# Three accumulator banks in turn for the samples' mLSTM state updates

## The chip, the cores and the metric

The kernel runs on one core of one Trainium2 chip. The metric is the device time of the kernel in microseconds, from the start of the launch to its end. The kernel before took 808.34 us, the median of three runs (807.4, 808.34 and 808.98).

## What is computed

One layer of a hybrid decoder, for a prompt of 256 tokens and for 8 samples of 8 new tokens each, in 32-bit floats. Each token goes through an mLSTM branch with 4 heads of 256 features and a forgetting-attention branch with 8 heads of 128. The branches are merged, and a mixture of 32 gated experts follows. The part that matters here is the mLSTM of the samples. Each of the 8 samples has, for each of the 4 heads, a state matrix C of 256 x 256 with a normaliser vector n beside it; the kernel holds the two as one 256 x 257 matrix, in two halves of 128 rows. The reference computes for it

```
num = w_inter[..., None] * jnp.einsum('bhtd,bhde->bhte', q, C) + jnp.einsum('bhts,bhse->bhte', s, v)
...
C_new = decay_state[..., None, None] * C + jnp.einsum('bhs,bhsd,bhse->bhde', w_rows, k, v)
```

That is, each of the 32 pairs of sample and head needs a query times state product, a key times value product (the update) and a read and a write of its state in memory.

## The kernel before, in words

Projections, attention and mLSTM pieces are interleaved by hand. The projections with `w_in` and the branch matrices are cut into 48 chunks of 256 columns and each chunk into 2 or 3 units; `dense` (lines 1808 to 1851) issues the matmuls of a unit. `stages()` (lines 74 to 137) attaches small pieces, called stages here, to units: after unit `(c, u)` each engine runs the stages in `AT[c, u]`, in the order of that list. PE, ACT and DVE each walk the same list in program order.

The samples' mLSTM consists of these stages, for head h and sample b:
- `SA(h)`: PE computes the scores of head h into bank 3 (`scores`, line 1934), DVE multiplies them by the decay weights (L1399), and ACT scales the keys (L989, L991) and masks them for the first sample (L998).
- `SB(h, b)`, called a step below, is numbered n = 8h + b. PE multiplies the masked queries by the sample's state and adds into bank 5 (L1995, two products). Then it computes the two halves of the update, into one bank each (L2006). DVE takes each half with one instruction, new state = decay x old state + bank (L1420), 128 x 257 elements each, and a tiny memset (L1422) signals that both are done. ACT masks the keys for the next step (L998), as soon as PE is through the step before.
- At the head's last sample, b = 7, PE also computes the scores times values product (L2001) between the two. ACT takes the upper half of bank 5 (L1008). DVE lays out the next head's queries (L1406), does its two L1420, adds the halves of bank 5 (L1425) and adds the product of L2001 (L1428).

The steps do not all come in a row: the 32 of them are spread over nine lines of the list, each behind one dense unit of the section `ga` (or the first unit of `gb`), with 4, 4, 3, 4, 3, 4, 3, 4 and 3 steps. `SA(h + 1)` follows `SB(h, 7)` directly, on every engine. The group of steps between two dense units is called a burst here. The first burst holds steps 0 to 3, the second 4 to 7, then 8 to 10, 11 to 14, 15 to 17, 18 to 21, 22 to 24, 25 to 28 and 29 to 31. Head ends (steps 7, 15 and 23, each followed by an `SA`) fall in bursts 2, 5 and 7; in bursts 5 and 7 the next head's first step follows in the same burst, in burst 2 a dense unit does. Burst 2 also holds the stages F2H and F2L of the prompt, which use bank 3 too.

PSUM has 8 banks. Dense units take banks 0 to 2 in turn, bank 3 holds scores, bank 5 query times state. PE claims a bank by waiting until its reader has let it go:

```
def claim(st, b):

    if fill[st, b]:
        pe.wait_ge(sem(f"bank_free{b}"), fill[st, b])
```

`fill[st, b]` is the number of earlier stages in the whole list that use bank b, counted from `banks_of(st)` (line 140). In `SB` the update banks are 6 and 7 for every step, and L2001 writes bank 4. `pe_past(st)` waits for the last bank in `banks_of(st)`.

The states move through rings in SBUF: four buffers `Cin` for the old states and four `Cout` for the new ones. All these transfers are issued on the POOL queue, 257 KB each: after step n (`cout_full`), first the load of the state for step n + 4 (L702) and then the store of the state of step n (L714). PE waits for the load at the head of a step (line 1993), DVE waits before step n + 4 until the store of n has landed (line 1414). The dense weights come on the SP queue, 1 MB a chunk.

Of the kernel before, what the change touches and what calls it, by code (L numbers as in the profile page):

```python
# [18 lines left out]
ALU = mybir.AluOpType  # L19
# [11 lines left out]
TP, BS, TS = 256, 8, 8  # L31
NS = BS * TS
# [3 lines left out]
HM, DM = 4, 256  # L36
DE = DM + 1
# [99 lines left out]
    return at  # L137


def banks_of(st):  # L140

    kind, x, y = st
    if kind == "G":
        return {1: (3,), 2: (4, 5, 6), 3: (3, 7), 4: (3, 7, 4, 5, 6), 5: (3,)}[x]
    if kind == "P2":
        return (4, 6, 7) if x == 0 else (5, 4, 6, 7)
    if kind == "SB":
        return ((5, 4) if y == BS - 1 else ()) + (6, 7)
    return {"KT": (6, 7), "P1": (3,), "F1": (), "F3": (), "F2": (6, 7), "F2H": (3,), "F2L": (), "SA": (3,), "N1": (), "N2": (6, 7),
            "FP1": (7, 4), "FP2": (5,), "FP3": (6,), "FS1": (3,), "FS2": (5,), "FS3": (3,), "FS4": (3,), "FS0": (),  # L150
            "FPN": (), "FSN": ()}[kind]
# [19 lines left out]
def hybrid_step(nc, A, O):  # L171
# [3 lines left out]
    for c in range(NCH):  # L175
        for u in range(units_of(c)):
            for st in AT[c, u]:
                for b in banks_of(st):
                    fill[st, b] = count[b]
                    count[b] += 1  # L180
    ctx = ExitStack()
    with ctx:
        handles = {}

        def sem(name):
            if name not in handles:
                
                handles[name] = ctx.enter_context(nc.semaphore(name))
            return handles[name]
# [15 lines left out]
        bank = [ctx.enter_context(nc.psum_tensor(f"bank{b}", [P, 512], F32)) for b in range(8)]  # L205
# [6 lines left out]
        def take(n):  # L212
            top[0] += n
            assert top[0] <= FW, top[0]
            return fm[:, top[0] - n:top[0]]

        def cube(ap, a):
            return ap.rearrange("p (a b) -> p a b", a=a)
# [18 lines left out]
        ew = cube(take(48), 3)  # L237
# [31 lines left out]
        num = cube(take(HM * DE), HM)  # L269
        qm = take(2 * BS * DIAG)  # L270
        SW = [take(128) for _ in range(2)]
        kw = [take(DM) for _ in range(2)]
        kwm = [take(DM) for _ in range(2)]
        inter = take(DE)
# [122 lines left out]
        def vx(t, h, w=DE):  # L397
            return vx01[:, t, h, 0:w] if t < 2 else vx2[0:NS, h, 0:w]
# [196 lines left out]
        def _(pool):  # L595
# [57 lines left out]
            def pe_past(st):  # L653

                b = banks_of(st)[-1]
                pool.wait_ge(sem(f"bank_full{b}"), fill[st, b] + 1)
# [168 lines left out]
        def _(act):  # L825
# [7 lines left out]
            def pe_past(st):  # L833

                b = banks_of(st)[-1]
                act.wait_ge(sem(f"bank_full{b}"), fill[st, b] + 1)
# [330 lines left out]
        def _(dve):  # L1167
            s = Steps(dve, sem("dve_step"))
            v = nc.vector
            TT, TSC, STT, CP = v.tensor_tensor, v.tensor_scalar, v.scalar_tensor_tensor, v.tensor_copy  # L1170

            def got(st, b):

                dve.wait_ge(sem(f"bank_full{b}"), fill[st, b] + 1)
# [6 lines left out]
            def done(ins, b):  # L1181
                s(ins, sem(f"bank_free{b}"))
# [221 lines left out]
            def lay_queries(h):  # L1404
                for k in range(2):
                    s(CP(diag(qm[:, 576 * k:576 * (k + 1)]), qT[:, 2 * h + k, TP:NT].rearrange("p (b t) -> p b t", t=TS)),  # L1406
                      sem("qm_full"))

            def SB(st):
                _, h, b = st  # L1410
                n = h * BS + b
                if n >= NCOUT:

                    dve.wait_ge(sem(f"cout_out{n % NCOUT}"), 16 * (n // NCOUT))
                if b == BS - 1 and h < HM - 1:
                    got(st, 5)
                    lay_queries(h + 1)
                for k, bk in enumerate((6, 7)):
                    got(st, bk)
                    done(STT(Cout[n % NCOUT][:, k, :], Cin[n % NCIN][:, k, :], dec8[:, HM * b + h:HM * b + h + 1],  # L1420
                             bank[bk][:, 0:DE], ALU.mult, ALU.add), bk)
                s(v.memset(small[0:1, 94:95], 0.0), sem("cout_full"))  # L1422
                if b == BS - 1:
                    dve.wait_ge(sem("inter_upper"), h + 1)
                    TT(inter[0:NS, :], bank[5][0:NS, 0:DE], inter[0:NS, :], ALU.add).then_inc(sem("bank_free5"), 1)  # L1425
                    dve.wait_ge(sem("bank_free5"), fill[st, 5] + 1)
                    got(st, 4)
                    done(STT(num[0:NS, h, :], inter[0:NS, :], ew[0:NS, 2, h:h + 1], bank[4][0:NS, 0:DE],  # L1428
                             ALU.mult, ALU.add), 4)
                    s(v.memset(small[0:1, 94:95], 0.0), sem("num_full"))  # L1430
                    s(v.memset(small[0:1, 94:95], 0.0), sem("inter_used"))

# [99 lines left out]
            def FS4(st):  # L1532
# [4 lines left out]
                s(v.memset(small[0:1, 94:95], 0.0), sem("o_full"))  # L1537

            run = dict(G=G, P1=P1, P2=P2, F1=F1, F2=F2, F2H=F2H, F2L=F2L, F3=F3, SA=SA, SB=SB, N1=N1, FP1=FP1,
                       FPN=FPN, FP3=FP3, FS0=FS0, FS1=FS1, FSN=FSN, FS2=FS2, FS3=FS3, FS4=FS4)  # L1540

# [254 lines left out]
        def _(pe):  # L1796
            mm = nc.tensor.matmul
            n_act = units(SECTIONS.index("bm") * CPS)[0]
# [6 lines that stand above are left out]
            def full(ins, b):  # L1805
                ins.then_inc(sem(f"bank_full{b}"), 1)
# [48 lines left out]
            for n in range(6):  # L1855
# [5 lines left out]
                for i in range(4):  # L1861
                    k = 4 * half + i
# [6 lines left out]
            for k in range(KC):  # L1869
                for i, (w, a) in enumerate(((0, 0), (0, 1), (1, 0))):  # L1870
                    ins = mm(bank[7][0:16, 0:NT], wgs[w][:, k, :], r1[a][:, k, :], start=(k == 0 and i == 0),
                             stop=(k == KC - 1 and i == 2))
# [114 lines left out]
            def SB(st):  # L1987
                _, h, b = st
                n = h * BS + b
                if b == 0:  # L1990
                    claim(("SB", h, BS - 1), 5)
                    pe.wait_ge(sem("qm_full"), 2 * (h + 1))
                pe.wait_ge(sem(f"cin_in{n % NCIN}"), 16 * (n // NCIN + 1))
                for k in range(2):
                    ins = mm(bank[5][NS * k:NS * (k + 1), 0:DE], qm[:, 576 * k + 64 * b:576 * k + 64 * (b + 1)],  # L1995
                             Cin[n % NCIN][:, k, :], start=(b == 0), stop=(b == BS - 1), skip_group_check=True)
                if b == BS - 1:
                    full(ins, 5)
                    pe.wait_ge(sem("bank_free3"), fill[("SA", h, 0), 3] + 1)
                    claim(st, 4)  # L2000
                    full(mm(bank[4][0:NS, 0:DE], SW[(2 * HM + h) % 2][0:NS, 0:64], vx(2, h), start=True, stop=True), 4)  # L2001
                pe.wait_ge(sem("kwm_ready"), n + 1)
                for k, bk in enumerate((6, 7)):
                    claim(st, bk)
                    rows = slice(NS * k, NS * (k + 1))
                    full(mm(bank[bk][:, 0:DE], kwm[n % 2][rows, 0:P], vx2[rows, h, :], start=True, stop=True), bk)  # L2006
# [91 lines left out]
            def FS4(st):  # L2098
# [3 lines left out]
                full(nc.tensor.transpose(bank[3][:, 0:P], Ob, ident), 3)  # L2102

            run = dict(G=G, KT=KT, P1=P1, P2=P2, F2=F2, F2H=F2H, SA=SA, SB=SB, N2=N2, FP1=FP1, FP2=FP2, FP3=FP3,
                       FS1=FS1, FS2=FS2, FS3=FS3, FS4=FS4)
            def turn(cc):
# [49 lines left out]
            for t in range(3):  # L2156
# [12 lines left out]
               start=False, stop=True, skip_group_check=True).then_inc(sem("router_full"), 1)  # L2169
# [192 lines left out]
```

## Time and profile before

| | us |
|---|---|
| median of 3 runs | 808.34 |
| the profiled execution, whole | 806.17 |
| its span in the trace | 804.6 |
| PE matmuls busy in the span | 712.9 (89%) |
| DVE busy | 392.5 (49%) |
| ACT busy | 294.7 (37%) |

The table reads as one kernel with several stretches: the dense sections in front keep PE busy, the experts at the end stream 96 MB of weights. The samples' steps lie between 204.9 and 287.8 us of the span. In the rows further below, a row of a timeline has the start in us, the duration in us, engine, line, operation, what is written and read, and how often; in brackets stands how long the engine had been idle before and what ended that. Two or more instructions of one line are merged into one row. One matmul of 32-bit floats makes two records, so "x4" is two products.

### The profile page before, as it was taken

How to read it: one execution, taken by the hardware profiler on the slowest of the kernel's cores; microseconds unless marked ns; L12 is line 12 of the kernel's file. 1: busy time of each engine (PE TensorE's matmuls, PEld its weight loads, DVE VectorE, ACT ScalarE, POOL GpSimd, SP SyncE). 2: the span in 40 equal slices, each digit the busy share in tenths (PEclk: the TensorE clock that was granted, in tenths of full speed). 3: DMA queues.
4: the chain of work that ended last, by engine and by line, in shares of the span. 5: the costliest groups of instructions: out<-in, count | busy, mean ns of one | idle time of the engine just before them, and what ended most of it. 6: DMA issues, size and time to landing. Idle time of an engine off the chain costs nothing.

```text
span 804.6 us, 14412 instructions
## 1 busy us (share of the span) xinstructions
PE 712.9 (89%) x5462; PEld 570.0 (71%) x5462; DVE 392.5 (49%) x865; ACT 294.7 (37%) x530; POOL 141.1 (18%) x247
## 2 busy tenths in 40 slices
PE   2999899999999999898899999895999999887880
PEld 1799899999666689898788899784565555443430
DVE  3475423456755453848477768648632222111123
ACT  5433544365533354546433354435221111111110
POOL 6000100000343300042243110000113223121210
PEclk9999999999999999999999999996999999999996
DMA  5342443332899944372798748926999999999975
GB/s 200 105 156 107 143 158 105 115 109 93 264 253 263 249 140 164 106 237 95 261 320 280 253 152 362 380 99 237 358 419 419 419 419 418 421 418 420 419 324 207
DMA packets 38186, 202.57 MB, mean 252 GB/s; under 512 B 7443, under 2 KB 7971, under 8 KB 18915
## 3 DMA queue, kind: packets, MB, share of 16 engines
q1 hardware_dynamic: 23938, 158.98, 51.2%
q0 software_dynamic: 13744, 41.32, 16.5%
q10 hardware_dynamic: 432, 1.31, 0.4%
q8 instruction: 46, 0.75, 0.4%
q14 instruction: 26, 0.21, 0.1%
HBM read 184.24 MB, written 23.12 MB: 258 GB/s over the span
## 4 chain that ended last, share of the span: by engine, by line
PE 65%; DMA 14%; DVE 12%; ACT 5%; issue 3%; SPq 1%; DVEq 0%; ACTq 0%; POOL 0%; POOLq 0%
PE bank L1844 22%; PE bank L1848 10%; PE bank L2208 9%; DMA fm<-in_w_moe 7%; PE bank L2228 4%; PE bank L1834 4%; DMA em<-in_w_moe 4%; DVE rm L1187 3%; PE bank L2006 2%; ACT rm L846 2%; PE bank L2092 1%; PE bank L1995 1%; PE bank L2180 1%; DMA fm<-y_rows 1%; DMA out_C_sample<-fm 1%
## 5 line engine op out<-in xcount | busy, mean ns | idle before, releaser
L1844 PE MATMUL bank<-rm 128*128 128x320 f32 x1344 | 206.0, 311 | 2.6 <-ACT fm L874 1.6
L1844 PEld LDWEIGHTS bank<-rm 128*128 128x128 f32 x1344 | 197.4, 188 | 7.3 <-issue 3.9
L1187 DVE TENSOR_TENSOR rm<-fm,rm 128x2048 fp32r<-128x2048 f32 x48 | 110.1, 2293 | 70.4 <-ACT rm L846 69.8
L1848 PE MATMUL bank<-rm 128*128 128x256 f32 x960 | 120.8, 284 | 2.4 <-DVE fm L1586 2.4
L1848 PEld LDWEIGHTS bank<-rm 128*128 128x128 f32 x960 | 116.9, 191 | 3.3 <-issue 2.9
L2208 PE MATMUL bank<-fm,em 128*64 128x256 f32 x368 | 93.7, 401 | 17.5 <-DMA fm<-in_w_moe 15.3
L846 ACT ACTIVATE rm<-fm 128x2048 fp32r<-128x2048 f32 x48 | 92.1, 1919 | 16.8 <-PE bank L1844 10.6
L2208 PEld LDWEIGHTS bank<-fm,em 128*64 128x64 f32 x368 | 49.5, 142 | 53.7 <-issue 31.5
L2210 PE MATMUL bank<-fm,em 128*64 128x256 f32 x320 | 82.6, 405 | 0.0
L1145 ACT ACTIVATE fm<-bank 64x256 f32<-64x256 f32 x32 | 12.0, 376 | 137.1 <-PE bank L2210 137.1
L778 POOL DMA_INDIRECT y_rows<-fm,im x32 | 28.9, 903 | 166.1 <-DVE fm L1741 166.1
L702 POOL DMA_DIRECT2D fm<-in_state_C x32 | 17.6, 551 | 164.4 <-DVE fm L1341 119.2
L2210 PE MATMUL bank<-em 128*64 128x256 f32 x192 | 46.3, 384 | 0.0
L2210 PEld LDWEIGHTS bank<-fm,em 128*64 128x64 f32 x320 | 43.3, 143 | 0.0
L1746 DVE TENSOR_TENSOR fm<-bank,fm 64x256 f32<-64x256 f32 x32 | 13.6, 426 | 60.7 <-ACT fm L1145 60.7
L1834 PE MATMUL bank<-rm 128*128 128x256 f32 x320 | 42.9, 286 | 0.0
L1420 DVE SCALAR_TENSOR_TENSOR fm<-fm,bank 128x257 f32<-128x257 f32 x64 | 28.0, 480 | 30.1 <-PE bank L2006 28.8
L1762 DVE COPY fm<-bank 128x128 f32<-128x128 f32 x32 | 9.3, 292 | 65.2 <-PE bank L2219 65.2
L1834 PEld LDWEIGHTS bank<-rm 128*128 128x128 f32 x320 | 40.0, 191 | 1.7 <-DVE fm L1586 1.0
L2208 PE MATMUL bank<-em 128*64 128x256 f32 x144 | 34.6, 383 | 2.8 <-DMA em<-in_w_moe 2.8
L2228 PE MATMUL bank<-em,fm 128*64 128x512 f32 x144 | 34.0, 593 | 1.5 <-issue 0.9
L1741 DVE COPY fm<-bank 64x512 f32<-64x512 f32 x32 | 22.2, 694 | 26.9 <-PE bank L2228 26.9
(400 smaller groups left out, 942.2 us busy)
## 6 DMA issues: line engine op xcount, KB each, us to landing
fm<-in_w_moe SPq DMA_DIRECT2D x57, 1024.0 KB, 22.1
fm<-in_w_dense SPq DMA_DIRECT2D x48, 1024.0 KB, 4.9
em<-in_w_moe SPq DMA_DIRECT2D x39, 1024.0 KB, 27.3
fm<-in_state_C POOLq DMA_DIRECT2D x32, 257.0 KB, 5.6
out_C_sample<-fm POOLq DMA_DIRECT2D x32, 257.0 KB, 6.7
fm<-in_cache_kT POOLq DMA_DIRECT2D x16, 512.0 KB, 6.8
fm<-in_cache_v POOLq DMA_DIRECT2D x8, 512.0 KB, 5.7
em<-in_cache_v POOLq DMA_DIRECT2D x8, 512.0 KB, 7.8
```

What stands on the lines that cost most here:

```text
L702: pool.dma_start(Cin[n % NCIN], A["state_C"][n % BS, n // BS]).then_inc(sem(f"cin_in{n % NCIN}"), 16)
L778: pool.indirect_dma_start(y_rows, bass.IndirectOffsetOnAxis(ap=row_i[:, v:v + 1].bitcast(U32), axis=0), yrow[v % NY], None, bounds_check=6 ...
L846: s(A_(pair[c % 2][0], cube(raw[c % RAW1], KC), ACT.Copy), sem("hi_done"))
L1187: s(TT(pair[c % 2][1], cube(raw[c % RAW1], KC), pair[c % 2][0], ALU.subtract), sem("split_done"))
L1420: done(STT(Cout[n % NCOUT][:, k, :], Cin[n % NCIN][:, k, :], dec8[:, HM * b + h:HM * b + h + 1], bank[bk][:, 0:DE], ALU.mult, ALU.add), bk)
L1741: CP(yrow[v % NY][:, D // 2:D], bank[4 + v % 2][CAP:2 * CAP, :]).then_inc(sem("e_y_right"), 1)
L1834: ins = mm(bank[b][:, 0:CW], samp[:, k, :], w[:, k, :], start=(k == 0 and i == 0), stop=(k == KC - 1 and i == 1))
L1844: ins = mm(bank[b][:, 0:NT], w[:, k, P * u:P * (u + 1)], a[:, k, :], start=first, stop=final)
L1848: ins = mm(bank[b][0:r, 0:CW], a[:, k, TILE0[u]:TILE0[u] + r], w[:, k, :], start=first, stop=final)
L2208: last_g = mm(bank[b][0:CAP, 0:FE], x[:, k, :], g[:, k, :], start=(k == 0), stop=(k == KC - 1), skip_group_check=True)
L2210: last_u = mm(bank[b][CAP:2 * CAP, 0:FE], x[:, k, :], u[:, k, :], start=(k == 0), stop=(k == KC - 1), skip_group_check=True)
L2228: ins = mm(bank[b][CAP * j:CAP * (j + 1), :], hT[:, k, :], w[:, k, 512 * j:512 * (j + 1)], start=(k == 0), stop=(k == 1), skip_group_check ...
```

## The change

In `banks_of` and in the `SB` of PE and DVE, the update of step n takes banks (6, 7), (4, 6) or (7, 4), by n modulo 3. The score times value product of a head's last step goes to bank 3 in place of bank 4. Nothing else is changed: the same instructions, sizes, transfers and order.

```diff
@@ -137,6 +137,11 @@
+def update_banks(h, b):
+
+    return ((6, 7), (4, 6), (7, 4))[(h * BS + b) % 3]
...
@@ -145,7 +150,7 @@
     if kind == "SB":
-        return ((5, 4) if y == BS - 1 else ()) + (6, 7)
+        return ((5, 3) if y == BS - 1 else ()) + update_banks(x, y)
...
@@ -1415,7 +1420,7 @@
-                for k, bk in enumerate((6, 7)):
+                for k, bk in enumerate(update_banks(h, b)):
                     got(st, bk)
...
@@ -1424,9 +1429,9 @@
-                    got(st, 4)
-                    done(STT(num[0:NS, h, :], inter[0:NS, :], ew[0:NS, 2, h:h + 1], bank[4][0:NS, 0:DE],
-                             ALU.mult, ALU.add), 4)
+                    got(st, 3)
+                    done(STT(num[0:NS, h, :], inter[0:NS, :], ew[0:NS, 2, h:h + 1], bank[3][0:NS, 0:DE],
+                             ALU.mult, ALU.add), 3)
...
@@ -1997,10 +2002,10 @@
                 if b == BS - 1:
                     full(ins, 5)
                     pe.wait_ge(sem("bank_free3"), fill[("SA", h, 0), 3] + 1)
-                    claim(st, 4)
-                    full(mm(bank[4][0:NS, 0:DE], SW[(2 * HM + h) % 2][0:NS, 0:64], vx(2, h), start=True, stop=True), 4)
+                    claim(st, 3)
+                    full(mm(bank[3][0:NS, 0:DE], SW[(2 * HM + h) % 2][0:NS, 0:64], vx(2, h), start=True, stop=True), 3)
                 pe.wait_ge(sem("kwm_ready"), n + 1)
-                for k, bk in enumerate((6, 7)):
+                for k, bk in enumerate(update_banks(h, b)):
                     claim(st, bk)
```

## Rows read from the trace of the kernel before

**Rows 1.** Window of all steps: length, PE, PEld, DVE, ACT, POOL busy, clock, DMA share, GB/s.
```profile
204.90:287.80 82.90, 78.53 (x478) 50.82 (x477) 46.66 (x135) 34.00 (x63) 32.02 (x59) 1.00 0.90 255
```

**Rows 2.** Waits of PE in that stretch: us in total, times, longest.
```profile
PE bank L1995 <- DVE fm L1425: 2.4, 2, 1.3
PE bank L2006 <- DVE fm L1420: 1.0, 6, 0.2
```

**Rows 3.** Timeline of PE, the third burst (steps 8 to 10).
```profile
226.12 0.65 PE L1995 MATMUL bank<-fm 128*64 128x257 f32 x4
226.70 0.70 PE L2006 MATMUL bank<-fm 64*128 64x257 f32 x4
227.34 0.65 PE L1995 MATMUL bank<-fm 128*64 128x257 f32 x4
228.16 1.00 PE L2006 MATMUL bank<-fm 64*128 64x257 f32 x4 [0.17 <-DVE fm L1420]
229.09 0.65 PE L1995 MATMUL bank<-fm 128*64 128x257 f32 x4
```

**Rows 4.** Timeline of DVE, the first of these steps.
```profile
227.53 0.88 DVE L1420 SCALAR_TENSOR_TENSOR fm<-fm,bank 128x257 f32<-128x257 f32 x2 [2.86 <-PE bank L2006]
```

**Rows 5.** Timeline of PE: the first step, and the dense unit behind each burst.
```profile
204.88 0.66 PE L1995 MATMUL bank<-fm 128*64 128x257 f32 x4
...
210.77 3.79 PE L1844 MATMUL bank<-rm 128*128 128x320 f32 x24
...
222.40 3.79 PE L1844 MATMUL bank<-rm 128*128 128x320 f32 x24
...
230.52 3.79 PE L1844 MATMUL bank<-rm 128*128 128x320 f32 x24
...
240.19 3.79 PE L1844 MATMUL bank<-rm 128*128 128x320 f32 x24
...
250.40 3.79 PE L1844 MATMUL bank<-rm 128*128 128x320 f32 x24
...
260.06 3.79 PE L1844 MATMUL bank<-rm 128*128 128x320 f32 x24
...
279.25 3.78 PE L1844 MATMUL bank<-rm 128*128 128x320 f32 x24
...
287.73 4.46 PE L1848 MATMUL bank<-rm 128*128 128x256 f32 x35
```

**Rows 6.** Timeline of DVE at the first head's end, and of PE there.
```profile
223.72 0.47 DVE L1428 SCALAR_TENSOR_TENSOR fm<-fm,bank 64x257 f32<-64x257 f32 x1
...
222.02 0.45 PE L1934 MATMUL bank<-fm 128*64 128x64 f32 x4
```

**Rows 7.** Busy time by window: before that head end.
```profile
211.50:224.40 12.90, 12.20 (x80) 8.13 (x80) 11.82 (x31) 7.98 (x13) 5.27 (x10) 1.00 0.96 280
```

**Rows 8.** Timeline at the second and third head's end: DVE and PE.
```profile
245.56 0.43 DVE L1406 COPY fm<-fm 128x64 f32<-128x64 f32 x2 [4.09 <-DMA out_C_sample<-fm]
...
247.41 0.47 DVE L1428 SCALAR_TENSOR_TENSOR fm<-fm,bank 64x257 f32<-64x257 f32 x1
...
247.43 0.65 PE L1995 MATMUL bank<-fm 128*64 128x257 f32 x4 [1.28 <-DVE fm L1425]
...
268.37 0.65 PE L1995 MATMUL bank<-fm 128*64 128x257 f32 x4 [1.13 <-DVE fm L1425]
```

**Rows 9.** Issue to landing: all stores (L714), then the load of step 14 (L702).
```profile
DMA to landing us min/median/max: 3.3/6.7/9.2
...
L702 POOL DMA_DIRECT2D fm<-in_state_C x1: 546/546/546, 231.7 to 231.7; - x1
DMA to landing us min/median/max: 7.0/7.0/7.0
```

**Rows 10.** Busy time, granted clock and DMA share by window: two quarters of the stretch.
```profile
226.00:247.00 21.00, 19.74 (x120) 12.72 (x118) 9.74 (x28) 8.23 (x17) 7.58 (x14) 1.00 0.91 247
268.00:288.00 20.00, 19.28 (x116) 12.57 (x117) 9.62 (x28) 6.80 (x12) 7.03 (x13) 1.00 0.79 234
```

## The prediction, made before the changed kernel was run

> **What bounds the kernel now.** I read the window of the steps first [rows 1]: of 82.9 us PE is busy in 78.5, at full clock, while DVE has 46.7 and ACT 34.0. So this stretch goes by PE, and what follows it is dense work on PE, so a microsecond won at its end should move all that comes later. But the same row has the 16 DMA engines busy for a share of 0.90. The second thing to see is that there are two suspects, PE's waits and the state transfers.
>
> The waits of PE [rows 2] name DVE's L1420, the reader of banks 6 and 7, with only 1.0 us in 6 waits. That is too small: a wait between the two products of a step hides in a longer "busy" row. The timeline shows it [rows 3]. Step 8 finds both banks free: 0.58 us from its start to its L2006 (226.12 to 226.70), 0.64 more to the next step, so a plain step is 1.22 us. Step 9 takes 1.75 us (227.34 to 229.09): its L2006 starts 0.24 us later than plain and is 1.00 us long in place of 0.70. DVE starts on the first bank 0.83 us after that L2006 started (226.70 to 227.53), is through both at 228.41, and PE goes on 0.63 us after DVE's start, at 228.16 [rows 3, 4].
>
> How much is that over all bursts? A dense unit holds PE for 3.72 us (230.52 to 234.24, where burst 4 starts), so a burst's length is the difference of two dense rows less 3.72 [rows 5]. Burst 1: 210.77 - 204.88 = 5.89 for 4 steps, against 4.88 plain: 1.01 held. Burst 3: 230.52 - 222.40 - 3.72 = 4.40 against 3.66: 0.74. Burst 4: 9.67 - 3.72 = 5.95 against 4.88: 1.07. Burst 5, behind the head's end at 247.43 [rows 8], 2.97 against 2.44 for 2 steps: 0.53. Burst 6: 9.66 - 3.72 = 5.94: 1.06. Burst 8 starts one plain step and one dense unit behind 268.37 [rows 8], at 273.31, and ends at 279.25: 1.06. Burst 9: 287.73 - 282.97 = 4.76 against 4.23 (a head's last step is 0.57 longer, for L2001): 0.53. Bursts 2 and 7 have no hold by these banks. Sum: **6.0 us**, all on PE's path.
>
> **Part 1, three banks.** Step n + 1 takes first a bank that step n doesn't use, then the first bank of step n. PE has that one back 0.83 + 0.63 = 1.46 us after step n's L2006 started [rows 3, 4], and wants it at 1.22 + 0.32 (half of the 0.64) = 1.54. It fits, by 0.1 us. Step n + 2 wants step n's second bank at 2.44; it is free at 0.83 + 0.88 + about 0.15 = 1.86. DVE has 0.88 us of work per step of 1.22. ACT's mask for step n + 2 starts when step n is through. So I take all 6.0 us of holds as removed, with 0 to 6.0 as ends. No instruction is added.
>
> **Part 2, bank 3, is a new wait.** Before, L2001's product lay in bank 4, and SA of the next head, right behind on PE, wrote its scores to bank 3, long free. Now SA's `claim` counts this use of bank 3 too: PE can't issue L1934 until DVE has read the product in L1428, the last of DVE's reading work for the head, behind L1406, both L1420 and L1425. Queued behind on PE are a dense unit (head 0) or the next head's first step (heads 1 and 2). Head 3 has no SA behind it.
> - Head 0: PE's L1934 started at 222.02, L1428 ended at 223.72 + 0.47 = 224.19 [rows 6]. DVE was busy 11.8 of the 12.9 us before [rows 7], so its end can't be drawn forward by PE; it starts this run of work 0.7 us earlier, though, since burst 1 is 1.0 us shorter (the square root on ACT in between keeps the rest). L1428 ends at 223.5, L1934 starts at 223.6: PE is **1.6 us later** than before. The hold of burst 1 is swallowed by this too: PE's earlier arrival only waits longer.
> - Heads 1 and 2: PE already waited there for bank 5, let go by L1425, until 247.43 and 268.37 (1.28 and 1.13 us idle, [rows 8]). L1428 ends at 247.41 + 0.47 = 247.88; then L1934 still has to run, 0.38 us (222.02 to 222.40, [rows 5, 6]), and only then the next step: 248.36 in place of 247.43, **0.93 us later**, twice. Between nothing (if the old wait covered it) and 1.3 us (all DVE's tail), I take 0.93, since the order on both queues is fixed.
>
> **Part 3, the transfers answer.** A load for step n + 4 is issued when step n is done, and lands 7.0 us later for step 14 (issued at 231.7, so at 238.7 [rows 9]; it is the last step of burst 4, which ends at 240.19 [rows 5], so it could hardly begin before). Bursts shorter by 1.0 us eat that slack. In burst 3 PE starts 1.6 later and ends 1.6 - 0.74 = 0.84 later; the load for step 14 goes out about 1.0 later and lands at 239.7, where a plain burst 4 wants it at 230.52 + 0.84 + 3.72 + 3 x 1.22 = 238.74. So burst 4 gives its gain back: it ends at 239.7 + 1.22 = 240.94, 0.75 later than before in place of 0.2 earlier. Next, DVE's L1406 at head 1's end waited for the store of step 11 (4.09 us, [rows 8]), which now goes out 0.84 later: DVE is 0.84 late there, and the step behind it 0.84 + 0.93 = 1.8 late, 0.1 more than PE's own sum.
>
> The sum, as PE's lateness against before: +1.6 after head 0, +0.84 after burst 3, +0.75 after burst 4, +1.75 behind head 1's end, +1.2 after the rest of burst 5 (-0.53), +0.15 after burst 6 (-1.06), +1.1 behind head 2's end, 0.0 after burst 8 (-1.06), **-0.5** at 287.7 (-0.53). Behind it nothing is changed. The profiled execution was 806.17 us; this makes 805.7, and against the median, 808.34, 2.2 us above it, **807.9 us**.
>
> **A rule weighed.** The trace has the same hold in 7 of 9 bursts on the engine that should be saturated [rows 3, 5]. The Trainium skill (Perfetto Trace Analysis, Optimization Strategy) says that a gap which repeats so can mean too little PSUM for the next tile. By it the change would be worth the whole 6.0 us; the trace agrees on the cause, and the new wait on bank 3 is what the rule doesn't see. On the transfers, the row has 3.3 to 9.2 us from issue to landing for 257 KB [rows 9]. The Trainium skill (DMA: Bandwidth & Descriptors, Anatomy of one DMA) gives 2.0 us and the size over 436 GB/s, an estimate of 2.6 us alone. The trace doesn't agree, since the queue is full here; by that figure part 3 would be nothing and the forecast 1.0 us lower.
>
> **The rivals.** 0.2% of this time, 1.6 us, is about what a measurement of this kernel can tell from no change.
> - *The transfers keep up*, because the share of 0.91 to 0.79 [rows 10] leaves room: only parts 1 and 2. From the +1.6 after head 0: -0.74 - 1.07 + 0.93 - 0.53 - 1.06 + 0.93 - 1.06 - 0.53 = -1.5, so 806.8 us. Add that DVE's tail at the head ends comes earlier than I think, by 0.3 each, and it is 2.4 us faster, 805.9. For it: the share falls to 0.79 at the end. Chance 0.2.
> - *All 6.0 us of holds come through*, 802.3 us: this needs DVE to have done L1428 before PE reaches the SA, and [rows 6, 8] show it 2.2 us (224.19 against 222.02) behind. The rule on repeating gaps above would have it so. Chance 0.02.
> - *The state queue sets the pace*, slower than before: 514 KB a step, with the share at 0.91 [rows 10] and landings up to 9.2 us [rows 9] against four buffers. Then bursts 4 to 6 gain nothing, since each step waits for the load issued four steps earlier, and the three head ends stand: 1.6 + 0.93 + 0.93 - 0.74 - 1.06 - 0.53 = +1.1 with bursts 3, 8 and 9 still gaining, +1.9 without burst 3, so 809.4 to 810.2 us. It decides from landings that are 0.5 us later, after their issue, than before. Chance 0.18.
> - *The change doesn't do what it says*: the fit of 0.1 us fails, a step is still held by DVE. Then L1428 ends at 224.19 as before, and PE is 2.2 late at head 0: 2.2 + 0.93 + 0.93 = +4.1, 812.4 us. Chance 0.03.
>
> **How the numbers follow.** The forecast's own case has 0.57, with 807.0 to 808.9. Beyond the 1.6 us on the fast side lies about half and a little more of the first rival, the second, and a few hundredths of the forecast: faster 0.2. On the slow side the last rival, half of the one on the state queue and a few hundredths: slower 0.17. Same 0.63. The range for 8 in 10 takes in most of the first rival and most of the state queue's: 806.2 to 809.9.
>
> **What would show it.** In the changed profile L2006 of every step should be 0.70 us and the steps of bursts 1, 3 and 6 1.22 us apart. PE should be idle 1.5 to 2.2 us before L1934 at head 0's end and 1.8 at the other two, released by L1428. Burst 4 should have a wait of about 1 us for a state load, and DVE's wait for a store at head 1's end should stay near 4 us. Rows of L2006 of 1.00 us would refute part 1; an L1934 that doesn't wait for L1428, part 2; a burst 4 of 4.9 us, part 3. A stretch that ends before 286 would make the number wrong.

## The result, and the profile of the changed kernel

The changed kernel takes **819.43 us** (median of 4 runs, 817.78 to 821.72), against 807.87 for the kernel before in the same session. The ratio is 1.014, with an interval of 1.0115 to 1.0165: 11.6 us slower, where no measurable change was forecast. The profiled execution took 819.31 us, its span 817.8; in the text below every difference between traces is between single executions.

The stretch of the steps grew from 82.85 us (204.88 to 287.73, [rows 5]) to 94.64 (204.26 to 298.90), by 11.8. So the loss lies there. Behind it the changed trace is 2.0 us longer as well (518.9 against 516.9 us to the end of the span): it has one more stretch of low clock, 42 us behind the steps, that the other trace lacks. In front it is 0.6 us shorter. The two profiled executions are 13.1 us apart, the medians 11.6. First the timeline of PE in the changed kernel (start, duration, engine, line, operation, count, idle time and its end in brackets). Its lines are 5 higher than before: L2000 is the query times state product, L2011 the update, L1939 the next head's scores, L1849 and L1853 dense units.

```profile
204.26 0.65 PE L2000 MATMUL bank<-fm 128*64 128x257 f32 x4
204.85 0.70 PE L2011 MATMUL bank<-fm 64*128 64x257 f32 x4
205.48 0.66 PE L2000 MATMUL bank<-fm 128*64 128x257 f32 x4
206.07 0.82 PE L2011 MATMUL bank<-fm 64*128 64x257 f32 x4
...
209.37 3.79 PE L1849 MATMUL bank<-rm 128*128 128x320 f32 x24
...
220.33 0.70 PE L2011 MATMUL bank<-fm 64*128 64x257 f32 x4 [0.56 <-ACT fm L1003]
223.31 0.69 PE L1939 MATMUL bank<-fm 128*64 128x64 f32 x4 [2.28 <-DVE fm L1433]
223.93 6.03 PE L1849 MATMUL bank<-rm 128*128 128x320 f32 x24
229.89 0.66 PE L2000 MATMUL bank<-fm 128*64 128x257 f32 x4
...
233.69 3.78 PE L1849 MATMUL bank<-rm 128*128 128x320 f32 x24
...
241.84 0.65 PE L2000 MATMUL bank<-fm 128*64 128x257 f32 x4 [0.57 <-DMA fm<-in_state_C]
...
251.68 0.39 PE L1939 MATMUL bank<-fm 128*64 128x64 f32 x3 [3.04 <-DVE fm L1433]
...
255.58 4.07 PE L1849 MATMUL bank<-rm 128*128 128x320 f32 x24
259.58 0.65 PE L2000 MATMUL bank<-fm 128*64 128x257 f32 x4
...
264.74 3.79 PE L1849 MATMUL bank<-rm 128*128 128x320 f32 x24
...
270.69 0.65 PE L2000 MATMUL bank<-fm 128*64 128x257 f32 x4 [0.94 <-DMA fm<-in_state_C]
...
276.88 0.58 PE L1939 MATMUL bank<-fm 128*64 128x64 f32 x3 [4.33 <-DVE fm L1433]
...
279.51 5.59 PE L1849 MATMUL bank<-rm 128*128 128x320 f32 x24
285.04 0.65 PE L2000 MATMUL bank<-fm 128*64 128x257 f32 x4
...
290.20 3.78 PE L1849 MATMUL bank<-rm 128*128 128x320 f32 x24
...
298.90 1.33 PE L1853 MATMUL bank<-rm 128*128 128x256 f32 x9
```

Three things are to be seen. The bursts are shorter: the first takes 209.37 - 204.26 = 5.11 us, where it took 5.89 [rows 5], and the third 233.69 - 229.89 = 3.80 in place of 4.40. Then L1939 stands behind DVE's L1433 for 2.28, 3.04 and 4.33 us, where PE was idle for 0, 1.28 and 1.13 [rows 8]. And the next dense unit takes 6.03, 4.07 and 5.59 us in place of 3.79, for the same 24 records; at the second and third head end a step or two stand between the wait and the unit.

The windows of the changed kernel behind the three waits say why (length, busy time of PE, PEld, DVE, ACT and POOL, then granted clock, DMA share, GB/s):

```profile
223.30:230.00 6.70, 6.69 (x30) 6.38 (x32) 0.34 (x3) 0.00 (x0) 0.37 (x1) 0.58 0.72 155
251.60:256.40 4.80, 4.72 (x23) 2.34 (x24) 1.94 (x9) 2.31 (x2) 1.52 (x3) 0.64 0.60 143
276.80:285.00 8.20, 8.12 (x36) 6.55 (x36) 3.52 (x8) 0.00 (x0) 1.52 (x3) 0.59 0.56 141
```

The granted clock is 0.58, 0.64 and 0.59 of full speed: PE ran for most of each at 1.2 GHz in place of 2.4, where the kernel before had 1.00 over the whole stretch [rows 1]. What happened before each fall was an idle PE.

DVE's side at the third head end of the changed kernel:

```profile
270.56 1.00 DVE L1425 SCALAR_TENSOR_TENSOR fm<-fm,bank 128x257 f32<-128x257 f32 x2 [4.89 <-DMA out_C_sample<-fm]
271.50 0.06 DVE L1427 MEMSET fm<- 1x1 f32 x1
274.41 0.43 DVE L1411 COPY fm<-fm 128x64 f32<-128x64 f32 x2 [2.85 <-issue]
274.87 0.88 DVE L1425 SCALAR_TENSOR_TENSOR fm<-fm,bank 128x257 f32<-128x257 f32 x2
275.80 0.06 DVE L1427 MEMSET fm<- 1x1 f32 x1
275.89 0.42 DVE L1430 TENSOR_TENSOR fm<-bank,fm 64x257 f32<-64x257 f32 x1
276.35 0.47 DVE L1433 SCALAR_TENSOR_TENSOR fm<-fm,bank 64x257 f32<-64x257 f32 x1
```

DVE waits for the store of step 18 to land, then idles 2.85 us more, put down to "issue". The kernel makes DVE wait there for the store of step 19. It was issued at 264.07 and landed 10.3 us later, at 274.4, which is when DVE goes on. All of DVE's tail (2.4 us) is behind that, and PE's scores behind the tail.

**Where the 11.8 us came from.** From the last L2011 of a head to the step behind the next dense unit: 9.56 in place of 4.73 us at head 1's end (220.33 to 229.89 against 221.39 to 226.12), 11.65 against 9.06 at the second, 13.19 against 7.14 at the third: 13.5 in all. Of that, idle time before L1939 or the next step is 9.65 - 2.41 = 7.2, and the rest, 6.2, together with 0.5 of bank holds that went, is the low clock: 6.58 for L1939 and a dense unit in place of 4.10, 7.90 in place of 6.54 for the second, 8.16 in place of 5.32 for the third, 6.7 in all. Waits of PE for state loads cost 0.6, 1.0 and 0.75 us in bursts 4, 7 and 9, against 0.1. The other bursts gave back 4.4 us. 13.5 + 2.4 - 0.1 - 4.4 leaves 0.4 of the 11.8 for small moves in burst 2.

### The profile page after: what moved, and what is told of

It reads as the page before. It is cut to its first block, busy times and chain, and to the rows that moved or that the text cites. A ratio compares the mean times of both kernels' runs of the same rounds, so it can differ in the third digit from the quotient of the medians.

```text
span 817.8 us, 14412 instructions
## 1 busy us (share of the span) xinstructions
PE 717.2 (88%) x5462; PEld 573.3 (70%) x5462; DVE 393.2 (48%) x865; ACT 294.5 (36%) x530; POOL 140.9 (17%) x247
## 4 chain that ended last, share of the span: by engine, by line
PE 64%; DMA 15%; DVE 11%; ACT 4%; issue 3%; SPq 1%; POOL 1%; DVEq 0%; ACTq 0%; POOLq 0%
PE bank L1849 21%; PE bank L1853 11%; PE bank L2213 9%; DMA fm<-in_w_moe 7%; PE bank L2233 4%; PE bank L1839 4%; DMA em<-in_w_moe 3%; DVE rm L1192 2%; DMA out_C_sample<-fm 2%; ACT rm L851 2%; PE bank L2097 1%; PE bank L2011 1%; PE bank L2185 1%; PE bank L2000 1%; DMA fm<-y_rows 1%
## 5 line engine op out<-in xcount | busy, mean ns | idle before, releaser
L1849 PE MATMUL bank<-rm 128*128 128x320 f32 x1344 | 210.3, 316 | 2.6 <-ACT fm L879 1.6
L1849 PEld LDWEIGHTS bank<-rm 128*128 128x128 f32 x1344 | 201.7, 192 | 8.0 <-issue 4.5
L1853 PE MATMUL bank<-rm 128*128 128x256 f32 x960 | 122.4, 287 | 2.4 <-DVE fm L1591 2.4
L1853 PEld LDWEIGHTS bank<-rm 128*128 128x128 f32 x960 | 118.4, 194 | 3.3 <-issue 2.9
L2213 PE MATMUL bank<-fm,em 128*64 128x256 f32 x368 | 92.4, 397 | 17.4 <-DMA fm<-in_w_moe 15.3
L851 ACT ACTIVATE rm<-fm 128x2048 fp32r<-128x2048 f32 x48 | 92.1, 1919 | 17.3 <-PE bank L1849 10.5
L2215 PE MATMUL bank<-fm,em 128*64 128x256 f32 x320 | 81.2, 400 | 0.0
L1839 PEld LDWEIGHTS bank<-rm 128*128 128x128 f32 x320 | 40.0, 191 | 1.7 <-DVE fm L1591 1.0
```

Of the source, the lines that this page charges most:

```text
L851: s(A_(pair[c % 2][0], cube(raw[c % RAW1], KC), ACT.Copy), sem("hi_done"))
L1839: ins = mm(bank[b][:, 0:CW], samp[:, k, :], w[:, k, :], start=(k == 0 and i == 0), stop=(k == KC - 1 and i == 1))
L1849: ins = mm(bank[b][:, 0:NT], w[:, k, P * u:P * (u + 1)], a[:, k, :], start=first, stop=final)
L1853: ins = mm(bank[b][0:r, 0:CW], a[:, k, TILE0[u]:TILE0[u] + r], w[:, k, :], start=first, stop=final)
L2213: last_g = mm(bank[b][0:CAP, 0:FE], x[:, k, :], g[:, k, :], start=(k == 0), stop=(k == KC - 1), skip_group_check=True)
L2215: last_u = mm(bank[b][CAP:2 * CAP, 0:FE], x[:, k, :], u[:, k, :], start=(k == 0), stop=(k == KC - 1), skip_group_check=True)
```

## The experiments

They ran in three sessions; each ratio is to the kernel before in the same one, so differences between runs of different sessions are best taken from the ratios. The last two columns are of the one profiled execution: its time, and the length of its stretch from the first step to the dense unit behind the last. Where that execution lies far from the median (it was the slowest of its kernel in e2, e5 and e11), the length says less about the median.

| run | us | ratio (interval) | profiled, us | stretch, us |
|---|---|---|---|---|
| the change | 819.43 | 1.014 (1.0115 to 1.0165) | 819.31 | 94.6 |
| e1 product in bank 3, two update banks | 814.46 | 1.0075 (1.0058 to 1.0092) | 813.70 | 90.0 |
| e2 three update banks, product apart | 807.40 | 0.9988 (0.9972 to 1.0003) | 810.24 | 83.6 |
| e3 change, scores a step earlier | 809.43 | 1.0029 (1.0002 to 1.0057) | 807.31 | 83.2 |
| e4 change, PE kept busy in the waits | 809.60 | 1.0026 (1.0004 to 1.0048) | 809.64 | 85.4 |
| e5 change, half stores | 810.12 | 1.0036 (1.0016 to 1.0055) | 814.50 | 89.2 |
| e6 before, half stores | 806.76 | 0.9981 (0.9965 to 0.9997) | 808.23 | 82.7 |
| e7 three banks, product apart, half stores | 803.96 | 0.9952 (0.9932 to 0.9972) | 804.45 | 80.2 |
| e8 as e2, PE kept busy at head ends | 806.89 | 0.9986 (0.9965 to 1.0006) | 807.22 | 83.0 |
| e9 as e4, first head end only | 811.18 | 1.0052 (1.003 to 1.0074) | 809.99 | 86.2 |
| e10 change, stores on SP | 815.39 | 1.011 (1.0073 to 1.0146) | 814.50 | 90.3 |
| e11 before, stores on SP | 806.57 | 1.000 (0.9983 to 1.0017) | 812.26 | 87.4 |
| e12 as e2, stores on SP | 806.95 | 1.0004 (0.9983 to 1.0024) | 806.99 | 82.7 |

### Each part alone: e1 and e2

e1 undoes the first part of the change:

```diff
 def update_banks(h, b):
-    return ((6, 7), (4, 6), (7, 4))[(h * BS + b) % 3]
+    return (6, 7)
```

> Only the second part of the change: the updates stay in banks 6 and 7 in turn, the score times value product goes to bank 3. Theory A (the slowdown is PE's wait at the three head ends for the product's reader, DVE's last instruction, plus the half granted clock that follows a wait of over 2 us): the loss stays, without the gain of three banks, so 816 to 825 us, with waits of L1939 on L1433 of 2 to 4 us at the head ends and a granted clock near 0.5 behind at least two of them. Rival B (three update banks, or bank 4 itself, disturb the bursts): as before the change, 807 to 810 us.

Measured: ratio 1.0075, so the loss is there with the second part alone, though smaller than expected (814.46 us, under the 816 that was the lower end). Its waits of L1939 and the windows behind them:

```profile
224.16 0.69 PE L1939 MATMUL bank<-fm 128*64 128x64 f32 x4 [2.15 <-DVE fm L1433]
224.78 6.13 PE L1849 MATMUL bank<-rm 128*128 128x320 f32 x24
...
252.50 0.39 PE L1939 MATMUL bank<-fm 128*64 128x64 f32 x3 [2.01 <-DVE fm L1433]
...
256.22 4.27 PE L1849 MATMUL bank<-rm 128*128 128x320 f32 x24
...
275.17 0.39 PE L1939 MATMUL bank<-fm 128*64 128x64 f32 x3 [2.02 <-DVE fm L1433]
...
276.62 3.79 PE L1849 MATMUL bank<-rm 128*128 128x320 f32 x24
```
```profile
224.00:231.00 7.00, 6.84 (x30) 6.54 (x32) 0.44 (x4) 0.00 (x0) 0.52 (x1) 0.57 0.60 169
252.50:256.50 4.00, 4.00 (x21) 1.87 (x22) 1.35 (x7) 2.31 (x2) 1.45 (x3) 0.68 0.52 139
275.00:280.40 5.40, 5.23 (x38) 4.32 (x40) 3.62 (x8) 1.55 (x1) 1.61 (x3) 1.00 0.82 200
```

The waits are 2.0 to 2.15 us at all three head ends, and the clock falls behind two of them. The third is as long as the second, and there the clock stays at 1.00. The stretch is 7.1 us longer than before.

e2 is the first part alone. The product needs a place where nothing waits for it: the upper 64 partitions of bank 3, since the scores use the lower 64. The Trainium skill (PSUM — Partial Sum Buffer, PSUM bank collisions raise a hardware error) says that two engines may use one bank at a time if they are in different groups of 32 partitions; no run here tests where that ends, but this one relies on it.

```diff
-                    claim(st, 3)
-                    full(mm(bank[3][0:NS, 0:DE], SW[(2 * HM + h) % 2][0:NS, 0:64], vx(2, h), start=True, stop=True), 3)
+                    if h == 0:
+                        pe.wait_ge(sem("bank_free3"), fill[("F2H", 1, 1), 3] + 1)
+                    else:
+                        pe.wait_ge(sem("num_full"), 2 * HM + h)
+                    mm(bank[3][NS:2 * NS, 0:DE], SW[(2 * HM + h) % 2][0:NS, 0:64], vx(2, h), start=True, stop=True)
...
-        return ((5, 3) if y == BS - 1 else ()) + update_banks(x, y)
+        return ((5,) if y == BS - 1 else ()) + update_banks(x, y)
```

DVE reads `bank[3][NS:2 * NS, 0:DE]`.

> Only the first part: three update banks in turn, and the product in the upper 64 partitions of bank 3, where the next head's scores don't have to wait for it. Theory A: no wait of L1939 on L1433, no half clock, and most of the 6.0 us of holds gone: 802 to 806 us. Rival B (bank rotation disturbs): 815 to 820 us. Rival C (the state transfers set the pace in any case): 806.5 to 809 us, with waits of PE for state loads and of DVE for stores that grow by what the holds lose.

Measured: 0.9988. The loss is gone, so three banks and bank 4 do no harm by themselves. But the 6 us aren't there either; that is rival C. PE in e2, where L1999 is the query times state product:

```profile
242.14 0.65 PE L1999 MATMUL bank<-fm 128*64 128x257 f32 x4 [0.26 <-DMA fm<-in_state_C]
...
246.44 1.12 PE L1999 MATMUL bank<-fm 128*64 128x257 f32 x4 [2.07 <-DVE fm L1430]
...
264.96 0.65 PE L1999 MATMUL bank<-fm 128*64 128x257 f32 x4 [0.74 <-DMA fm<-in_state_C]
...
286.02 0.65 PE L1999 MATMUL bank<-fm 128*64 128x257 f32 x4 [1.13 <-DMA fm<-in_state_C]
```

PE waits 2.4 us in all for state loads, and the old wait for bank 5 at the second head end is 2.07 us in place of 1.28 (DVE waits for a store ahead of it, as before the change), with a granted clock of 0.58 over the 4 us behind it. The clock fell once more at 287.3, 1.3 us behind the start of the row at 286.02, ahead of which PE had waited 1.13 us for a load. This trace is of the slowest of ten executions; the median is 2.8 us lower.

The two parts don't add: the second alone costs 0.75%, the first alone nothing, both 1.4%.

### The order alone: e3

```diff
+            if b == BS - 1 and h < HM - 1:
+                line.append(("SA", h + 1, 0))
             line.append(("SB", h, b))
...
-        if h < HM - 1:
-            line.append(("SA", h + 1, 0))
```

> The whole change, but the next head's scores (SA) are put ahead of the head's last step in the hand-written order, so that they no longer stand behind the product in bank 3. Theory A: as the run with the product apart, 802 to 806 us; a short wait of PE for bank 3 ahead of the product (up to 0.5 us, three times) is possible. Rival B: 815 to 820 us. Rival C: 806.5 to 809 us.

Measured: 1.0029. All of the change is kept but the scores' place, and 9 of the 11.6 us come back. It isn't the 802 to 806 of theory A: PE now waits for bank 3 ahead of the product, 2.0 us in 2 waits (behind DVE's L1404), more than the 0.5 each that I had allowed, and twice for bank 5, 1.50 and 1.60 us. Behind the second of these the granted clock was 0.61 for 4.1 us. The ten executions spread more than those of other runs, from 805.63 to 815.38 us; the profiled one, at 807.31, is among the fast.

### The clock: e4, e9 and e8

In e4 PE computes something that nobody reads while it would wait, into the bank that the next dense unit overwrites:

```diff
             def SA(st):
                 _, h, _ = st
+                if h:
+                    c, u = at_unit
+                    n = units(c)[0] + u + 1
+                    m = n - NRING
+                    pe.wait_ge(sem("unit_free_a"), m + 1 - thirds(m))
+                    for _ in range((3, 4, 4)[h - 1]):
+                        mm(bank[n % NRING][:, 0:NT], ident, fm[:, 0:NT], start=True, stop=True)
                 claim(st, 3)
```

> The whole change, with 3, 4 and 4 matmuls that nobody reads (128x320, about 0.6 us each) on PE ahead of the wait at the three head ends, so that PE is busy while it would be idle. They compute nothing of the output. Theory A (both wait and clock count): the wait itself stays, the granted clock stays at full level, and the 6.7 us that the trace shows lost at the lower level come back: 811 to 814 us. Theory A' (only the wait counts, the clock fell for another reason): 818 to 821 us, with the clock still at half behind the head ends. If the wait for the product were not the cause, more work on PE would only add: 820 us or more.

Measured: 1.0026. With eleven added matmuls the kernel is 9.2 us faster by the ratios (809.60 against 819.43 us). Their record (L1995), the scores and the dense unit behind them at the first head end, and the windows at all three:

```profile
221.49 1.88 PE L1995 MATMUL bank<-fm 128*128 128x320 f32 x6
223.84 0.45 PE L1939 MATMUL bank<-fm 128*64 128x64 f32 x4 [0.47 <-DVE fm L1433]
224.21 3.79 PE L1849 MATMUL bank<-rm 128*128 128x320 f32 x24
```
```profile
221.50:228.00 6.50, 6.03 (x38) 4.95 (x38) 2.42 (x10) 1.37 (x4) 1.53 (x3) 1.00 0.94 306
247.00:256.00 9.00, 9.00 (x56) 6.42 (x56) 6.29 (x15) 3.79 (x6) 3.25 (x6) 1.00 0.61 161
267.80:275.60 7.80, 7.62 (x48) 5.73 (x46) 5.73 (x14) 3.33 (x5) 2.96 (x6) 1.00 0.70 171
```

PE still can't issue L1939 before L1433: it starts 19.05 us behind the first step in both traces. So the order costs what it did, but the clock is 1.00 and the dense unit 3.79 us. The gain is larger than the 6.7 us of low clock: at the other two head ends L1939 came within 0.2 us behind 2.42 us of such matmuls, where it had waited 3.04 and 4.33. So there is a follow-on.

e9 is e4 with `if h == 1` in place of `if h`, that is, at the first head end only.

> The whole change with the matmuls that nobody reads (3) only in the wait at the first head end; at the other two PE idles as in the changed kernel. If the late landings of the stores (waits of 3.0 and 4.3 us at heads 2 and 3 in place of about 2) come from what the low clock behind the first head end did to the bunching of the bursts: 811 to 813.5 us, waits of L1939 near 2.0 us at both. If they come from shorter bursts alone: waits of 3 us and more stay, 814 to 817 us.

Measured: 1.0052, by the ratios 7 us better than the change, by keeping one wait busy whose own low clock had cost 2.5. L1939 waits 3.04 us at the second head end, as in the change, and 2.10 at the third in place of 4.33; the clock is 0.61 behind the second and 1.00 behind the third. Neither expectation held whole: the time fits the first, the second wait the other. The late stores at the third head end went with the first fall of the clock, those at the second didn't. The fall alone doesn't make them late either: e1, with two update banks, has it too (0.57), and its third wait is 2.02 us.

e8 puts two such matmuls behind the scores at head ends 2 and 3 of e2.

> Three update banks with the product apart, whole stores, and at head ends 2 and 3 two matmuls that nobody reads (1.3 us) behind the next head's scores, where PE otherwise idled 2.1 and 1.2 us for bank 5 and the clock fell behind the first of these. The theory: no low clock in the stretch of the steps, about 1.5 us less than the run with the product apart: 805 to 807 us. If that fall of the clock cost nothing or has another cause: 807 to 809 us.

Measured: 0.9986, against 0.9988 for e2. The clock was full at both head ends, but fell once elsewhere, behind a wait of 1.55 us for a state load in burst 4. So 806.89 us lies in the expected range, but no gain over e2 is shown.

### The transfers: e5, e6 and e7

The three store only the first half of each new state:

```diff
-                pool.dma_start(O["C_sample"][n % BS, n // BS], Cout[n % NCOUT]).then_inc(sem(f"cout_out{n % NCOUT}"), 16)
+                pool.dma_start(O["C_sample"][n % BS, n // BS][:, 0, :], Cout[n % NCOUT][:, 0, :]).then_inc(sem(f"cout_out{n % NCOUT}"), 16)
```

> The changed kernel, with the store of each new state cut to its first half (128 rows x 257, 128.5 KB in place of 257); the second half is not written to memory. The theory (late landings of the stores make DVE late at head ends 2 and 3, so they lengthen PE's new wait from the 1.8 us that order alone gives to 3.0 and 4.3, and set off the low clock): waits of L1939 at heads 2 and 3 of 1.5 to 2.1 us, no wait of DVE for a store, 811 to 815 us; the first head's wait (2.3 us) and its low clock stay. If landings don't matter: waits as in the changed kernel, 817 to 820 us.

> The control: the kernel before, with the same halved stores. In its profile the stores' landing holds DVE 4.1 and 1.1 us and through it PE at two head ends by up to 1.3 us each. The theory: 805 to 807.5 us. If transfers were what sets the whole stretch: 803 us or less.

> Three update banks with the product apart (upper 64 partitions of bank 3), and halved stores. The theory (three banks do remove 6 us of holds on PE, but the transfers, near their limit, give them back as waits for loads and stores): now the gain shows, 800.5 to 804 us, 2.5 us or more under the kernel before with halved stores, with the waits of PE for state loads (2.4 us in 4 with whole stores) under 0.5 us. If the holds are given back elsewhere (DVE or ACT): 804.5 to 807 us.

Measured: e5 1.0036, e6 0.9981, e7 0.9952. In e5 no wait of DVE for a store is left, and L1939 waits 2.28, 2.02 and 2.11 us: order alone. The median, 810.12 us, is a little under the range. The profiled execution is the slowest of the ten, with the clock low behind all three waits (0.56, 0.66 and 0.75), so its stretch of 89.2 us is longer than most would be. The kernel before gains 0.2% by the same cut (e6), within what was expected if transfers don't set its stretch. And now three banks are worth something: e7 is 2.8 us under e6, with every run of it (802.79 to 804.56) under every run of e6 (804.58 to 808.28), no wait of PE for a load, and this burst 4 (start at 232.41, next dense unit at 237.57), 5.16 us for four steps:

```profile
232.41 0.66 PE L1999 MATMUL bank<-fm 128*64 128x257 f32 x4
...
237.57 3.79 PE L1848 MATMUL bank<-rm 128*128 128x320 f32 x24
...
264.62 0.93 PE L1999 MATMUL bank<-fm 128*64 128x257 f32 x4 [1.33 <-DVE fm L1430]
265.47 1.23 PE L2013 MATMUL bank<-fm 64*128 64x257 f32 x4
266.63 4.52 PE L1848 MATMUL bank<-rm 128*128 128x320 f32 x24
```

It lost some 1.5 us again to the clock, which fell behind a wait of 1.33 us for bank 5: from 264.62 the step and the dense unit take 6.46 us, where 1.22 + 3.72 is plain.

### Another queue: e10, e11 and e12

The stores are issued from SP, ahead of the load of the dense chunk that its program comes to after the same bursts:

```diff
+            def states_out(c):
+                for u in range(units_of(c)):
+                    for st in AT[c, u]:
+                        if st[0] == "SB":
+                            n = stored[0]
+                            sp.wait_ge(sem("cout_full"), n + 1)
+                            sp.dma_start(O["C_sample"][n % BS, n // BS], Cout[n % NCOUT])\
+                                .then_inc(sem(f"cout_out{n % NCOUT}"), 16)
+                            stored[0] += 1
...
             for c in range(RAW1, NCH):
+                if c - RAW1 >= 2:
+                    states_out(c - RAW1 - 2)
```

> The changed kernel with the stores of the new states issued from the SP queue, among the dense weights' loads, in place of the POOL queue, whose order held each load and store one behind the other. Same bytes. If the single POOL queue is what makes landings late: waits of DVE for stores under 2 us in all, L1939 waits near 2.0, 811 to 814 us. If the DMA engines themselves are full: 815 to 820 us.

> The kernel before with its stores on the SP queue: the control. Its head ends wait for a store once (4.1 us of DVE): 806 to 808 us if the queue is the cause of that, 807.5 to 810 us if the engines are full.

> Three update banks, the product apart in the upper 64 partitions of bank 3, and the stores on the SP queue: the candidate for a version faster than both. If the POOL queue's order is the limit: 803 to 806 us, as with halved stores. If the DMA engines are: 806.5 to 809 us, as with the stores on POOL.

Measured: 1.011, 1.000 and 1.0004. The waits only change places: DVE waits for no store in any of the three, but PE waits for state loads 3.5 us in 5 waits in e10 and in e12, and the median load of the stretch takes 6.6 us to land in e10, where it took 6.0 in the changed kernel. In e10 the wait for L1433 (the scores are L1953 there) is 2.28, 2.01 and 2.10 us, order alone, as the first branch expected; but the time is that of the second. The median is 4 us under the changed kernel's, with intervals that overlap (1.0073 to 1.0146, 1.0115 to 1.0165). So late stores leave DVE, but late loads come in their place, though the loads now have the POOL queue to themselves; cutting the bytes took both away. That speaks for what the DMA engines have to move in the time, and against the order of one queue, as the cause. Of the versions that write the whole states none beats the kernel before; e2, e8 and e12 are level with it.

## Why the prediction was wrong, point by point

The forecast was 807.9 us, within 806.2 to 809.9; measured were 819.43.

- **Part 1, three banks: right.** 6.0 us of holds were to go. Bursts 1, 3, 6 and 8 are 5.11, 3.80, 5.16 and 5.16 us, against 4.88, 3.66, 4.88 and 4.88 forecast: some 0.15 us are left in every second step ("0.85" in place of 0.70), so the margin of 0.1 us was not quite there. About 5 of the 6 us went.
- **Part 2, the new wait: place and order right, price wrong.** L1934 behind L1428 is where the loss is (e1, e2, e3). I had PE 1.6 us late at the first head end; counted from the first step it is 2.15, and the wait there is 2.28 idle us, just above the 1.5 to 2.2 that I had named. The failed step is "PE is 1.6 us later": it counted the wait and let the dense unit behind it take its 3.72 us. It took 6.03, because the granted clock fell to 1.2 GHz. The low clock took 6.7 us at the three head ends, a term that the sum didn't have. In the same way the two waits of "0.93 us later" cost 2.6 and 6.0, of which 1.4 and 2.8 are the clock and the rest the order itself and late stores (part 3). I read "at full clock" in the row of the stretch and never asked what PE's new idle time would do to it. In the stretch of the steps the trace of before had no wait of 2 us, only one of 1.28 us, which kept the clock. Further on, behind the steps, it had longer ones. Here are two of them, each with the window behind it (the clock is the third number from the end):

```profile
393.72 0.90 PE L2036 MATMUL bank<-fm 128*128 128x128 f32 x3 [2.87 <-DVE fm L1470]
...
393.70:398.00 4.30, 4.28 (x25) 3.55 (x29) 0.74 (x3) 0.57 (x2) 0.09 (x1) 0.61 0.98 403
...
511.53 3.10 PE L1848 MATMUL bank<-rm 128*128 128x256 f32 x24 [2.37 <-DVE fm L1586]
...
511.50:515.50 4.00, 3.97 (x32) 3.77 (x33) 2.57 (x7) 3.50 (x7) 0.00 (x0) 1.00 1.01 420
```

  Behind 2.87 idle us the granted clock was 0.61, behind 2.37 it stayed at 1.00, and so it did behind a wait of 2.04 us at 329.25. So the price could have been seen, as one that may or may not be charged, and the range should have had the low clock in it. The Trainium skill (TensorE: Matmul & The Clock Gate, HAM oscillation — how this bites in real kernels) tells of this: gaps in which PE waits for a DMA put it back to the lower clock for the work behind them. The changed trace agrees, with 0.58 of full speed behind 2.28 idle us, though PE waited for DVE there and not for a DMA.
- **Part 3, the transfers: right in kind, too small.** I had one load late by 1 us and one store by 0.84. Loads cost PE 2.4 us in three waits, and late stores made DVE late at both later head ends: L1939 waited 3.04 and 4.33 us, where order alone gives 2.0 to 2.1 (e1, e5). The bursts that part 1 shortened ask for the same 514 KB a step in less time, and stores took up to 10.5 us to land, against 9.2 before [rows 9]. So the gain of one part lengthens the wait of the other. "The queue is full here" was not borne out as a matter of the POOL queue: with the stores on another one the loads landed no sooner (e10).
- **The rivals.** None reached the measured time. The one on the slow side, with +1.1 to +1.9, had the later landings, but it wanted bursts 4 to 6 to gain nothing, and bursts 4 and 6 were 0.3 and 0.8 us shorter; it had no clock in it either. The first rival, that the transfers keep up, is excluded for whole stores by e2 and holds for half stores only (e7).
- **The sum.** How much later PE was than before, counted from the first step, at the dense unit behind each burst (from [rows 5] and the timeline of the changed kernel):

  | behind burst | forecast, us | measured, us |
  |---|---|---|
  | 2 (head 0 ends) | +1.6 | +2.15 |
  | 3 | +0.84 | +3.8 |
  | 5 | +1.2 | +5.8 |
  | 6 | +0.15 | +5.3 |
  | 8 | 0.0 | +11.6 |
  | 9 | -0.5 | +11.8 |

  The jumps stand where the clock is low and the stores are late. The 12.3 us between -0.5 and 11.8 are 6.7 for the clock, 1.0 and 2.3 for waits at the second and third head end beyond what order alone gives, 1.3 more for loads and about 1 for the 0.15 us left in the bursts, good to some tenths, since each comes from one trace.

What stays open: why the stores of steps 18 and 19 landed as late as they did. e9 ties those at the third head end to the fall of the clock at the first, in a kernel with three banks, with one execution each. I don't know how the one leads to the other; a shift of the bursts against the dense weights' loads would do it, but that wasn't tried.

## What to carry to other kernels

Moving a result into another buffer moves a wait: ask who writes that buffer next, and what its present reader still has to do first. On PE a wait costs more than its length where the clock falls behind it, as it did here behind three waits of 2.3 to 4.3 us; where one can't be avoided, matmuls that nobody needs in its place can be the cheaper idle. And a gain in a stretch whose transfers take most of the DMA engines' time may not show until there are fewer bytes to move, as here (e2 against e7).

## What the runs showed that I had not expected

- The clock fell behind a wait of PE of 1.33 us (e7), 1.55 (e8) and 1.60 (e3), and once behind one of 1.13 (e2). It did not behind 1.28 (before), 1.50 (e3), 2.10 (e9) or 2.37 us (before, at 511.53), and of two waits of 2.0 us in e1 one had it and the other not. So the length of one wait doesn't settle it, and what does is not shown here.
- Eleven useless matmuls of 0.6 us made a kernel of 819 us some 9 us faster.
- Halving the stores took the median landing of a load from 6.1 us (e2) to 4.5 (e7) with the same loads.
